# Expert weight tiles: SyncE's request for tile n also waits for the landing of tile n-4

## What is computed

```
h = silu(x @ w_gate[e]) * (x @ w_up[e])        # w_gate, w_up: 1024 x 256
y = h @ w_down[e]                              # w_down: 256 x 1024
out[token] += weight(token, e) * y             # two experts per token
```

## Time and profile before

| | |
|---|---|
| median of 3 runs | 1769.39 us (1766.47 to 1772.17) |
| span of the profiled execution | 1769.0 us, granted clock 0.981 |
| busy: TensorE matmuls, VectorE, ScalarE, GpSimd | 93%, 54%, 42%, 11% of the span |
| DMA queue of SyncE (q1) | 288.92 MB, 46.6% of 16 engines over the span |
| instruction queue q8 | 120 packets, 1.97 MB |

### The profile page before, as it was taken

The page is one execution under the profiler, slowest core; times in us unless marked ns, Lnnn a source line. Parts: engine busy times, 40 slices in busy tenths (PEclk is TensorE's granted clock), DMA queues, the critical chain, the costliest instruction groups (busy, mean ns, idle before and its releaser), DMA issues.

```text
span 1769.0 us, 37413 instructions
## 1 busy us (share of the span) xinstructions
PE 1638.5 (93%) x15037; PEld 1317.2 (74%) x15037; DVE 952.1 (54%) x1733; ACT 747.9 (42%) x1419; POOL 191.1 (11%) x287
## 2 busy tenths in 40 slices
PE   6888889986888998999999999999999999989997
PEld 6775679884666664886675788888885887879997
DVE  5743564687223224274756555335535565578685
ACT  6332445543111124335756333333335556555455
POOL 0020011031000001002422100000013002220001
PEclk9999999997999999999999999999999999999999
DMA  6597624479999996221014422222235440255552
GB/s 253 184 235 270 226 94 142 143 216 294 364 388 404 352 381 238 72 93 39 2 46 167 157 96 95 96 84 95 95 99 187 156 143 14 74 202 189 181 191 73
DMA packets 84420, 302.06 MB, mean 171 GB/s; under 512 B 10080, under 2 KB 12128, under 8 KB 84128
## 3 DMA queue, kind: packets, MB, share of 16 engines
q1 hardware_dynamic: 80144, 288.92, 46.6%
q0 software_dynamic: 2736, 7.35, 1.7%
q10 hardware_dynamic: 1376, 3.47, 0.5%
HBM read 345.56 MB, written 3.15 MB: 197 GB/s over the span
## 4 chain that ended last, share of the span: by engine, by line
PE 78%; DVE 10%; DMA 4%; issue 4%; ACT 3%; ACTq 0%; POOL 0%; SPq 0%; DVEq 0%
PE bank L1015 52%; PE bank L971 13%; PE bank L1585 5%; DMA ring<-wall 4%; PE bank L1620 3%; PE bank L1605 3%; PE bank L1039 2%; DVE w_lo L2397 2%; ACT w_hi L1850 1%; PE bank L1597 1%; PE bank L1641 1%; DVE SV L2445 1%; DVE BIG L2640 0%; DVE bank L2444 0%; DMA XC<-xin 0%
## 5 line engine op out<-in xcount | busy, mean ns | idle before, releaser
L1015 PE MATMUL bank<-BIG_f32r,w_hi 128*128 128x256 f32 (+1 forms) x2208 | 545.5, 336 | 5.1 <-DVE w_lo L2397 2.9
L2397 DVE TENSOR_TENSOR w_lo<-ring,w_hi 128x1024 fp32r<-128x1024 f32 x261 | 322.3, 1244 | 291.2 <-ACT w_hi L1850 289.6
L1015 PEld LDWEIGHTS bank<-BIG_f32r,w_hi 128*128 128x128 f32 x2208 | 375.4, 188 | 63.3 <-issue 15.5
L1015 PE MATMUL bank<-BIG_f32r,w_lo 128*128 128x256 f32 (+1 forms) x1136 | 381.6, 336 | 0.0
L1850 ACT ACTIVATE w_hi<-ring 128x1024 fp32r<-128x1024 f32 x261 | 272.4, 1053 | 192.0 <-PE bank L1015 154.7
L1015 PE MATMUL bank<-AR_f32r,w_hi 128*128 128x256 f32 (+1 forms) x1050 | 271.3, 333 | 2.2 <-DVE w_lo L2397 2.2
L1015 PEld LDWEIGHTS bank<-BIG_f32r,w_lo 128*128 128x128 f32 x1136 | 214.1, 188 | 24.9 <-issue 0.7
L1015 PEld LDWEIGHTS bank<-AR_f32r,w_hi 128*128 128x128 f32 x1050 | 181.7, 189 | 25.6 <-issue 6.3
L1015 PE MATMUL bank<-AR_f32r,w_lo 128*128 128x256 f32 (+1 forms) x440 | 145.7, 331 | 0.0
L1015 PE MATMUL bank<-XC_f32r,w_lo 128*128 128x256 f32 x424 | 122.7, 289 | 0.0
L1015 PE MATMUL bank<-XC_f32r,w_hi 128*128 128x256 f32 x424 | 122.7, 289 | 0.0
(11 more groups left out here) (402 smaller groups left out, 2319.7 us busy)
## 6 DMA issues: line engine op xcount, KB each, us to landing
ring<-wall SPq DMA_DIRECT2D x417, 512.0 KB, 4.3
BIG<-wall SPq DMA_DIRECT2D x90, 512.0 KB, 8.2
w_extra<-wall ACTq DMA_DIRECT2D x15, 2048.0 KB
w_extra<-wall ACTq DMA_DIRECT2D x15, 1024.0 KB
AR<-wall SPq DMA_DIRECT2D x20, 512.0 KB, 8.3
con<-wall SPq DMA_DIRECT2D x10, 512.0 KB, 8.3
lnst<-wall SPq DMA_DIRECT2D x6, 512.0 KB, 8.4
BIG<-t_rows POOLq DMA_DIRECT2D x16, 128.0 KB, 14.5
```

The costliest lines, as they stand in the source:

```text
L1015: ins = nc.tensor.matmul(o, l, r, start=start and n == 0, stop=stop and n == 2, **kw)
L2397: V.tensor_tensor(w_lo[:, i % SPLIT_RING, :], ring[:, t % RING, :], w_hi[:, i % SPLIT_RING, :].bitcast(F32), ALU.subtract).then_inc(w_spli ...
```

## The change

Each request of an expert tile waits, behind the wait for its slot, until the tile four places earlier in the stream has landed. At most four expert tiles are then under way. Nothing else is touched; for the first four expert tiles the tile waited for belongs to the stage before.

```
+MOE_IN_FLIGHT = 4
...
                     elif before is not None:
                         sp.wait_ge(w_free, whole_at[before] + 1)
+                    if in_moe:
+                        landed_in(sp, t - MOE_IN_FLIGHT)
                     sp.dma_start(slot(t), src).then_inc(w_ready[slot_at[t]], 16)
                     t += 1
```

## The result

The changed kernel takes 1779.99 us (median of 20 runs, 1771.69 to 1784.85); the kernel before takes 1771.20 us (median of 20, 1766.47 to 1776.21). The ratio is 1.005, with a 95% interval of 1.0039 to 1.0062: slower by about 9 us, where 1768 and "no change" were forecast. The profiled execution has a span of 1780.6 us at a granted clock of 0.979 (before: 1769.0 us, 0.981); from 460 to 610 us the clock is 0.99 in both, so the loss among the experts is not the clock's. SyncE's new wait is on L564, and what follows the two new pieces has moved by three lines: L843 is now L846, L1585 L1588, L1605 L1608, L1620 L1623.

What follows compares the result with a forecast made beforehand. The prediction took TensorE to set the experts' pace, with DMA engines just as full. SyncE wait 0, supply 0 and fetches -1 us on 1769.0 us gave 1768 us; own range 1765 to 1772, 8-in-10 range 1757 to 1775.

Steps and rivals of the forecast that it cites:

- no change: Whole kernel: the limit does nothing that can be felt, 1767 to 1771 us; chance 0.58.
- The added wait on SyncE: 0: SyncE's requests: one wait for each of 186 tiles delays no landing, even of the last expert tile; 0 us.
- Supply with four out: 0, bounded by +6 us: Expert weight stream: four tiles out keep the DMA engines full, a tile every 1.28 us; 0, at worst +6 us.
- So 5.1 - 3.3 = 1.8 us remain: Expert stream: place in line 5.1 us less lone landing 3.3 leaves SyncE 1.8 us before an engine runs dry.
- 1.44 us a tile: Expert stream between tiles 18 and 171: slowest supply before TensorE waits, 5.8 us for four tiles.
- rival 2: Expert stream: a tile waits for its slowest engine, quick ones run dry, 6 us slower, 1775 us; chance 0.13.
- its two signs: Experts' stage: DMA share under 0.95 before 600 us, and TensorE waiting for landing tiles at L1585.
- Instruction fetches: -1 us, between -10 and 0: TensorE's issue gaps in the experts, 21.3 us in all: fewer queued tiles save 1 us, at most about 10.
- Depth beyond four seems not to be what a fetch waits for: TensorE's instruction fetches: they wait while an engine is busy at all, whatever the tiles queued; gaps stay 0.6 to 0.8 us.
- Two fetches read singly: Gaps after fetches at 625.76 and 632.57 us, four or five tiles out: mean 0.77 us, no less than 0.71.
- the average of 0.44: Issue gap per fetch from 613 to 643 us, some 4.4 tiles out, against 0.71 with more than six.
- rival 1: Experts' stage: fetches do queue behind tiles, so fewer tiles shorten TensorE's gaps, 1759 to 1763 us; chance 0.29.

Runs made afterwards that it cites:

- twenty: The changed kernel with the wait for the tile twenty places earlier in place of four: 1768.15 us, ratio 0.9996 to the kernel before.
- the run with a third of the fetches: The changed kernel, four tiles out, with three quarters of up and scatter matmuls and half of down left out: 1769.53 us, one run.

## Why the prediction was wrong, point by point

**"The added wait on SyncE: 0"** holds for the wait: with twenty it costs nothing that can be measured. That the last expert tile would land at the same time does not hold: asked at 683.97 us, it lands at 689.6 (669.7 before), because the supply was slower.

**"Supply with four out: 0, bounded by +6 us"** is the step that failed. "So 5.1 - 3.3 = 1.8 us remain" takes the time of a lone tile for that of a tile among others. With two others out a tile already takes 5.1 us; the slack was about nothing. The step had the right test, 1.44 us a tile, and the supply came to 1.48. The +6 us rested on a median of four tiles and on the part after 613 us; the waits were 26.5 us and began at about 555, because TensorE, faster by its shorter gaps, spent its stock of landed tiles and the supply could not refill it. The step's own formula shows this: with 1.48 it gives 153 x (1.48 - 1.44) = 6 us again. But the limit of 1.44 was worked out for a TensorE with 21.3 us of gaps; without 17.4 of them tile 171 is needed that much sooner, the limit is (655.5 - 17.4 - 435.0) / 153 = 1.33, and the loss 153 x (1.48 - 1.33) = 23 us. The sum added up two terms that depend on each other. The mechanism stood in rival 2, in its own words: a tile waits for its slowest engine, one that has just carried a fetch, "and the quick ones run dry". It had a chance of 0.13, and its price of 6 us was too low. Of its two signs the waits at `moe_up` came; a share under 0.95 did not (0.97). The cost per fetch (0.87 us with four out, 0.05 to 0.2 with five or more) and the run with a third of the fetches tie the loss to the fetches, and the single steps of `w_ready` show that one engine holds back the landing. That it is the very engine which carried the fetch fits in time, but the trace does not name it.

**"Instruction fetches: -1 us, between -10 and 0"** was mis-sized too. "Depth beyond four seems not to be what a fetch waits for" holds above five (0.66 with six, 0.68 before), but at four the gaps fell by 17.4 us in the stage, past the bound of 10: up to 540 us, where TensorE waits for no tile, they are 0.19 us a fetch. That an engine with nothing in hand takes a fetch at once is the reading, not shown by itself. Two fetches read singly, 1.03 and 0.50 us, were weighed against the average of 0.44, and the average was nearer. So rival 1's gain was real, and came with rival 2's loss: while engines stand free for a fetch they move no weights. The prediction had also said where it would end: when the weights become the limit. They did from about 555 us on, only at 354 GB/s and not at 395.

Of the two rules weighed, the one from the Trainium skill's "DMA: Bandwidth & Descriptors", section "Queues, rings and completion order" (an engine takes its queues in turn, a packet of descriptors at a time), agrees with the runs at six out and without a limit, 0.42 to 0.71 us a fetch with no growth by depth. The forecast carried that over to four out, where the gaps up to 540 us are 0.19. "Runtime: NRT & Kernel Launch", section "Instruction fetch mechanics", says that the crossing of a block is mostly hidden: the traces come near it only with four out (0.19 us a fetch up to 540 us), not where weights fill the engines (0.66 to 0.71 there with six and more out).

**The range** of 1757 to 1775 ended below the median of 1779.99, since it took its upper bound from the 6 us.

## What to carry to other kernels

A limit on transfers in flight has to cover the round as it is under load, with the longest disturbance of a single engine on top: measure that round with two and three transfers out, as a lone one here is too short by 1.8 us. Read GB/s beside the DMA share: a share of 0.97 went with 354 GB/s, one of 1.00 with 395. When one term of a forecast makes an engine faster, work out the slack of the other terms for the faster engine. Where the consumer has a stock, a tighter limit can pay for as long as the stock lasts, since instruction fetches then come sooner: four out for 64 tiles and then five gave 0.9969 of the time before, though five throughout, at 0.9978 and 0.9986, can't be told from it.

## What the hardware showed unexpectedly

One 16 KB packet that holds one of sixteen DMA engines for about 1 us delays the whole stream by 0.87 us when four tiles of 0.524 MB are out, and by 0.05 to 0.2 us with five or more; with four out, in the sixteen landings that come latest after the one before, the last of the semaphore's sixteen steps follows the fifteenth by a median of 1.12 us. A tile's landing takes 3.3, 4.3 and 5.1 us with none, one and two others out, although with two and three tiles out the engines are busy only 0.77 and 0.90 of the time.
